# Modulation vectors on VectorE inside the second feed-forward, context work inside that stage and the mixer's

## The reference, cut to what matters

```python
x = x + jnp.square(jax.nn.relu(h @ w_ffn_up[l])) @ w_ffn_down[l]      # end of block 2
...
# start of block 3
sh1, sc1, g1, sh2, sc2, g2 = ada_split(c, w_ada[l], b_ada[l])          # silu(c) @ w_ada + b_ada, six vectors of 1024
csh1, csc1, cg1, csh2, csc2, cg2 = ada_split(c_ctx, w_ada[l], b_ada[l])
u_l, v_l, q_l, k_l, vv_l, o_l, gt_l = split_proj(modulate(x, sh1, sc1) @ w_in[l])
u_c, v_c, q_c, k_c, vv_c, o_c, gt_c = split_proj(modulate(xc, csh1, csc1) @ w_in[l])   # the context, 256 tokens
```

## Time and profile before

| | |
|---|---|
| median of three runs | 4226.23 us (4224.4 to 4230.27) |
| the profiled execution, its own time | 4218.46 us |
| its span, first to last instruction | 4216.7 us |
| mean granted TensorE clock | 0.952 |
| TensorE busy | 3840.2 us (91%) |
| VectorE busy | 2213.2 us (52%) |
| ScalarE busy | 1296.4 us (31%) |
| data moved | 218.14 MB, 52 GB/s on the mean |

### The profile page before, as it was taken

How to read it: one execution, slowest core, us unless ns; L and a number is a source line. 1 busy time by engine, 2 the same in 40 slices (tenths; PEclk the granted TensorE clock), 3 DMA queues, 4 the chain that set the end, 5 groups by cost and what they waited for, 6 DMA issues and landing times. The chain is left out here.

```text
span 4216.7 us, 45629 instructions
## 1 busy us (share of the span) xinstructions
PE 3840.2 (91%) x18134; PEld 3084.2 (73%) x18134; DVE 2213.2 (52%) x3153; ACT 1296.4 (31%) x1902; POOL 157.2 (4%) x95
## 2 busy tenths in 40 slices
PE   6988899999996798787999999988698989999997
PEld 5877778888884686566788888735597756888885
DVE  1087676777776793444434444412636565444446
ACT  1143252222224224434322222212522364222323
POOL 3310000000000000000000000000000000000000
PEclk9998999999998899888999999998899999999998
DMA  2110011111111011000111111162022200111111
GB/s 102 50 61 0 20 40 54 52 45 46 46 50 60 25 51 60 21 0 20 40 60 40 47 54 41 40 233 106 32 65 65 80 30 30 60 40 60 41 51 50
DMA packets 59044, 218.14 MB, mean 52 GB/s; under 512 B 4541, under 2 KB 17085, under 8 KB 53234
## 3 DMA queue, kind: packets, MB, share of 16 engines
q1 hardware_dynamic: 58290, 214.94, 14.1%
q10 hardware_dynamic: 576, 0.72, 0.0%
HBM read 202.97 MB, written 12.65 MB: 51 GB/s over the span
## 5 line engine op out<-in xcount | busy, mean ns | idle before, releaser
L1122 PE MATMUL psum<-mixer_r,pairs_r 128*128 128x512 f32 x2016 | 796.5, 395 | 36.0 <-DVE gemm_input_r L1398 19.4
L1123 PE MATMUL psum<-gemm_input_r,pairs_r 128*128 128x512 f32 x2016 | 788.2, 391 | 0.0
L1124 PE MATMUL psum<-mixer_r,pairs_r 128*128 128x512 f32 x2016 | 788.1, 391 | 0.0
L1156 PE MATMUL psum<-hidden_r,pairs_r 128*128 128x512 f32 x1376 | 543.0, 395 | 27.8 <-DVE residual L1468 13.0
L1157 PE MATMUL psum<-hidden_r,pairs_r 128*128 128x512 f32 x1376 | 539.1, 392 | 0.0
L1158 PE MATMUL psum<-hidden_r,pairs_r 128*128 128x512 f32 x1376 | 539.1, 392 | 0.0
L1468 DVE TENSOR_TENSOR residual<-residual,psum 128x512 f32<-128x512 f32 x592 | 384.0, 684 | 206.6 <-PE psum L1158 205.5
L1122 PEld LDWEIGHTS psum<-mixer_r,pairs_r 128*128 128x128 f32 x2016 | 380.9, 189 | 128.2 <-DVE pairs_r L1393 20.6
L1123 PEld LDWEIGHTS psum<-gemm_input_r,pairs_r 128*128 128x128 f32 x2016 | 381.2, 189 | 81.0 <-issue 2.9
L1124 PEld LDWEIGHTS psum<-mixer_r,pairs_r 128*128 128x128 f32 x2016 | 380.7, 189 | 79.9
L1231 ACT ACTIVATE pairs_r<-pairs 128x2048 fp32r<-128x2048 f32 (+1 forms) x108 | 187.1, 1736 | 793.1 <-DMA pairs<-in_w_up 385.0
(11 more groups left out here) (451 smaller groups left out, 5704.0 us busy)
## 6 DMA issues: line engine op xcount, KB each, us to landing
pairs<-in_w_up SPq DMA_DIRECT2D x38, 1024.0 KB, 7.1
pairs<-in_w SPq DMA_DIRECT2D x32, 1024.0 KB, 5.3
weight_slots<-in_w_ada SPq DMA_DIRECT2D x24, 1024.0 KB, 4.8
pairs<-in_w_down SPq DMA_DIRECT2D x16, 1024.0 KB, 5.2
pairs<-in_w_down SPq DMA_DIRECT2D x22, 512.0 KB, 3.2
pairs<-in_w_in SPq DMA_DIRECT2D x11, 1024.0 KB, 5.2
weight_slots<-in_w_in SPq DMA_DIRECT2D x10, 1024.0 KB, 4.8
pairs<-in_w_out SPq DMA_DIRECT2D x9, 1024.0 KB, 6.0
```

The source lines that it names most:

```text
L1122: pe.matmul(out, w_hi[:, at], c.MR[:, k, halves[n]], start=k == 0, stop=False)
L1123: pe.matmul(out, w_hi[:, at], c.HR[:, k, halves[n]], start=False, stop=False)
L1124: mm = pe.matmul(out, w_lo[:, at], c.MR[:, k, halves[n]], start=False, stop=k == KT - 1)
L1156: pe.matmul(bank, hi, hid(0, ch, n, kd), start=kd == 0, stop=False)
```

## The change

The vectors are made within the second feed-forward: for chunks 3 to 14, one group of 512 columns of `w_ada` each (12 groups), in two parts of 1 MB (four of the eight rows of 128 features). VectorE multiplies each 128 x 512 piece by one number per partition and adds it to an accumulator: four steps a part and vector. Groups 0 to 3 serve both vectors (8 steps a part), groups 4 to 11 only `c`'s (4 steps a part). From group 1 on the first part's steps stand behind the up slab's split, the second part's between the drains 4 to 7 of the first half. TensorE sums over the partitions against a column of ones (8 or 4 matmuls), ScalarE stores the result. The context is normalised in chunk 2, goes to DRAM and comes back at the end of the stage; modulation, gates, keys and values of it are made in the mixer's stage with the slabs that lie there for the latents, as sums of three products. Three stages and their DMAs are gone; `w_ada_3` is laid out by groups.

```diff
+        self.ctx_hi = over("ctx_hi", 47, [P, KT, CTX], F32R)
+        self.ctx_lo = over("ctx_lo", 44, [P, KT, CTX], F32R)
+        self.ctx_norm = nc.dram_tensor("ctx_norm", (P, KT * CTX), F32, kind="Internal").ap()
...
+class ContextSide:
+    FIRST, GROUPS, BOTH = 3, 12, 4
+    def __init__(self, c):
...
+        self.part = [a.rearrange("p a (b n) -> p (a b) n", n=HALF) for a in (c.norm_tiles[0], c.norm_tiles[1][:, 0:2, :])]
+        self.acc = [c.norm_tiles[1][:, 2, 0:HALF], c.norm_tiles[1][:, 2, HALF:]]
...
+        self.steps, at = [], 0
+        for g in range(self.GROUPS):
+            half = 8 if g < self.BOTH else 4
+            self.steps.append((at + half, at + 2 * half))
+            at += 2 * half
+    def group(self, ch):
+        g = ch - self.FIRST
+        return g if 0 <= g < self.GROUPS else None
+    def vectors(self, g):
+        return range(2 if g < self.BOTH else 1)
+    def load(self, sp, g, h):
+        w = self.c.inp["w_ada_3"][g * P:(g + 1) * P, h * SLAB:(h + 1) * SLAB].rearrange("p (k n) -> p k n", n=HALF)
+        sp.dma_start(self.part[h], w).then_inc((self.s["ada_a"], self.s["ada_b"])[h], 16)
+    def gemv(self, dve, g, h, ks=range(4)):
+        width = len(self.vectors(g))
+        n = self.steps[g][h] - (4 - ks[0]) * width
+        dve.wait_ge((self.s["ada_a"], self.s["ada_b"])[h], 16 * (g + 1))
+        if g and not h:
+            dve.wait_ge(self.s["summed"], g)
+        for k in ks:
+            for v in self.vectors(g):
+                w, by = self.part[h][:, k, :], self.cond[:, 4 * h + k, v:v + 1]
+                if k or h:
+                    dve.wait_ge(self.s["gemv"], n + 1 - width)
+                    dve.scalar_tensor_tensor(out=self.acc[v], in0=w, scalar=by, in1=self.acc[v], op0=ALU.mult,
+                                             op1=ALU.add).then_inc(self.s["gemv"], 1)
+                else:
+                    dve.tensor_scalar(self.acc[v], w, by, None, ALU.mult).then_inc(self.s["gemv"], 1)
+                n += 1
+    def sum_up(self, pe, g):
+        pe.wait_ge(self.s["gemv"], self.steps[g][1])
+        n = 4 * len(self.vectors(g))
+        for i in range(n):
+            mm = pe.matmul(self.c.PS[:, 0, i:i + 1], self.acc[i // 4][:, (i % 4) * P:(i % 4 + 1) * P], self.c.ones[:, 0:1],
+                           start=i == 0, stop=i == n - 1, skip_group_check=True)
+        mm.then_inc(self.s["summed"], 1)
+    def keep(self, act, g):
+        n = len(self.vectors(g))
+        act.wait_ge(self.s["summed"], g + 1)
+        act.activation(self.ada[:, 4 * g:4 * g + 4, 0:n], self.c.PS[:, 0, 0:4 * n].rearrange("p (s a) -> p a s", a=4),
+                       ACT.Copy).then_inc(self.s["ada_kept"], 1)
...
             for ch in range(2, N):
                 sp.wait_ge(up_done, up_at[ch - 2, 1, 1])
                 load_up(ch)
+                if side is not None and ch == 2:
+                    sp.wait_ge(A[1][0].s["scaled"], 8)
+                    sp.dma_start(side.x, c.inp["ctx"].rearrange("p (k n) -> p k n", n=CTX)).then_inc(s["ctx_in"], 16)
+                if side is not None and ch == 4:
+                    sp.wait_ge(s["ctx_scaled"], 1)
+                    side.load(sp, 0, 0)
+                    sp.dma_start(c.ctx_norm.rearrange("p (k n) -> p k n", n=CTX), side.sq).then_inc(s["ctx_out"], 16)
+                    sp.wait_ge(s["ctx_out"], 16)
+                    side.load(sp, 0, 1)
+                if side is not None and side.group(ch):
+                    g = side.group(ch)
+                    for h in range(2):
+                        sp.wait_ge(s["gemv"], side.steps[g - 1][h])
+                        side.load(sp, g, h)
...
+            if side is not None:
+                sp.wait_ge(up_done, up_at[E, 1, 1])
+                sp.dma_start(c.PW[:, 8:10, :], c.ctx_norm.rearrange("p (a n) -> p a n", n=T)).then_inc(c.ctx_landed, 16)
+                sp.wait_ge(c.ctx_landed, 16)
...
                 if ch >= 1:
                     pe.wait_ge(up_drained, up_at[ch - 1, n, m])
+                if side is not None and ch == 3 and m == 0:
+                    pe.wait_ge(s["ctx_log"] if n else s["ctx_centred"], 1)
+                if side is not None and ch > 3 and m == n == 0 and side.group(ch - 1) is not None:
+                    pe.wait_ge(s["ada_kept"], side.group(ch - 1) + 1)
...
+                if side is not None and ch == 2:
+                    pe.wait_ge(s["ctx_in"], 16)
+                    pe.wait_ge(up_drained, up_at[2, 0, 0])
+                    for k in range(KT):
+                        mm = pe.matmul(PS[:, 0, 0:CTX], c.ones_d[:, :], side.x[:, k, :], start=k == 0, stop=k == KT - 1)
+                    mm.then_inc(s["ctx_mean"], 1)
+                    down_half(1, 0)
+                    pe.wait_ge(s["ctx_sq"], 1)
+                    pe.wait_ge(up_drained, up_at[2, 1, 0])
+                    for k in range(KT):
+                        mm = pe.matmul(PS[:, 1, 0:CTX], c.ones_d[:, :], side.sq[:, k, :], start=k == 0, stop=k == KT - 1)
+                    mm.then_inc(s["ctx_sums"], 1)
+                    down_half(1, 1)
+                elif side is not None and side.group(ch) is not None:
+                    down_half(ch - 1, 0)
+                    down_half(ch - 1, 1, range(0, 4))
+                    pe.wait_ge(up_drained, up_at[ch, 0, 0])
+                    side.sum_up(pe, side.group(ch))
+                    down_half(ch - 1, 1, range(4, 8))
+                elif not conv:
...
+                    if side is not None and ch == 2:
+                        for v, name in enumerate(("c_3", "c_ctx_3")):
+                            act.activation(side.cond[:, :, v:v + 1], c.vec(name, 0, 8).unsqueeze(2),
+                                           ACT.Silu).then_inc(s["cond_ready"], 1)
                     round_slab("up", ch + 1)
                     evacuate(ch, 0, 0)
                     round_slab("down", ch - 1)
                     evacuate(ch, 0, 1)
                     evacuate(ch, 1, 0)
                     evacuate(ch, 1, 1)
+                    if side is not None and ch == 2:
+                        act.preload_act_table_set("natural_log_exp_and_others")
+                        act.wait_ge(s["ctx_centred"], 1)
+                        act.activation(side.sq, side.x, ACT.Square).then_inc(s["ctx_sq"], 1)
+                        act.wait_ge(s["ctx_sums"], 1)
+                        act.activation(side.rstd, PS[:, 1, 0:CTX], ACT.Ln, bias=c.ln_eps[:, :]).then_inc(s["ctx_log"], 1)
+                        act.wait_ge(s["ctx_log"], 1)
+                        act.activation(side.rstd, side.rstd, ACT.Exp, scale=-0.5).then_inc(s["ctx_rstd"], 1)
+                    if side is not None and side.group(ch) is not None:
+                        side.keep(act, side.group(ch))
...
+                    g = None if side is None else side.group(ch)
                     split_slab("up", ch + 1)
+                    if g:
+                        side.gemv(dve, g, 0)
                     low_hidden(ch, 0, 0)
                     split_slab("down", ch - 1)
                     low_hidden(ch, 0, 1)
                     low_hidden(ch, 1, 0)
+                    if g == 0:
+                        dve.wait_ge(s["cond_ready"], 2)
+                        side.gemv(dve, g, 0)
+                    if side is not None and ch == 2:
+                        dve.wait_ge(s["ctx_mean"], 1)
+                        mean = PS[:, 0, 0:CTX].unsqueeze(1).to_broadcast([P, KT, CTX])
+                        dve.tensor_tensor(side.x, side.x, mean, ALU.subtract).then_inc(s["ctx_centred"], 1)
                     drains(ch - 1, 0, range(0, 3))
                     low_hidden(ch, 1, 1)
-                    drains(ch - 1, 0, range(3, 8))
-                    drains(ch - 1, 1)
+                    for m in range(3, 8):
+                        drain(ch - 1, 0, m)
+                        if g and m >= 4:
+                            side.gemv(dve, g, 1, range(m - 4, m - 3))
+                    if g == 0:
+                        side.gemv(dve, g, 1)
+                    drains(ch - 1, 1, range(0, 4))
+                    if side is not None and ch == 2:
+                        dve.wait_ge(s["ctx_centred"], 1)
+                        dve.wait_ge(s["ctx_rstd"], 1)
+                        rstd = side.rstd.unsqueeze(1).to_broadcast([P, KT, CTX])
+                        dve.tensor_tensor(side.sq, side.x, rstd, ALU.mult).then_inc(s["ctx_scaled"], 1)
+                    drains(ch - 1, 1, range(4, 8))
             if not conv:
                 split_slab("down", E - 1)
+            if side is not None:
+                dve.wait_ge(s["ada_kept"], side.GROUPS)
...
-def block3_ada(c, prefetch):
...
-def block3_context(c, prefetch):
...
-    units = [("gate", 0, n) for n in range(2)]
-    units += [(w, m, n) for w in "qk" for m in range(2) for n in range(2)]
-    units += [(w, t) for w in ("vals0", "vals1", "v0") for t in range(NC_)]
```

(75 more changed lines are left out.)

156 lines of the change are left out of this document (40 added, 116 removed).

## The result

The changed kernel takes **4109.02 us** (median of four runs, 4106.36 to 4114.25), the kernel before in the same session 4227.85 (4224.4 to 4230.27): a ratio of **0.9721, with a 95% interval of 0.9704 to 0.9738**. The forecast was 4121, range 4103 to 4142. The profiled execution of the changed kernel took 4110.98 us with a span of 4109.2, that of the kernel before 4218.46 and 4216.7. So the spans differ by -107.5 us where the sum said -105.0, and the medians by -118.8.

The account below looks back on a forecast made before the run. TensorE, busy 91% of the span, was taken as the bound; -153.5 + 0.6 + 6.9 + 16.6 + 3.2 + 21.2 = -105.0 us gave 4113.5 us, and 7.8 from execution to median gave 4121 us, range 4103 to 4142.

Parts of the forecast that it names:

- Removed stages: Between feed-forward and the latents' layer norm: three stages go, boundaries included, -153.5 us.
- Chunks: Second feed-forward: TensorE's added context statistics, sums, clock loss and group 0's lateness, +27.3 us.
- the sum over partitions: Feed-forward chunks: 128 one-column TensorE instructions at 0.13 us each, 16.6 us, between 7.7 and 27.
- a clock that should fall behind two of the four long sums: Feed-forward chunks with two vectors: TensorE's clock falls behind two of four sums, 3.2 us.
- VectorE's steps and its margins: Feed-forward chunks: steps of 0.66 to 0.79 us lie beside TensorE, costing 0, with 1.5 us of cover; group 0 excepted.
- rival C: Feed-forward chunks: VectorE holds TensorE up, about 10 us over four chunks at 1.0 us a step, 4131 us; chance 0.12.
- Rival B: Feed-forward chunks: the clock falls behind every sum, 19.2 us in place of 3.2, 4137 us; chance 0.10.
- Rival E: Feed-forward, SyncE's queue: late second parts delay the next slabs in every chunk, slower than before, 4241 us; chance 0.02.
- Rival D: Feed-forward sums: small matmuls at their lower bound and no clock fall, 8.9 + 3.2 us better, 4109 us; chance 0.12.
- Layer norm: The latents' layer norm stage after the feed-forward: no change expected, 0 us.
- Mixer: Mixer stage: context units 20.2 us, later gate split 1.2, cheaper evacuation -0.2, together +21.2 us.
- VectorE modulates eight tiles, 0.3 us each: Mixer's start: eight 128 x 256 modulation steps ahead of the gate slab's split make it 1.2 us later.

Follow-up runs that it names:

- second profile: The changed kernel run and profiled once more with no edit, the base for the small edits: 4108.84 us, ratio 0.9732 to the kernel before.
- the doubled sum: Every sum over partitions computed twice in the changed kernel: 4131.88 us in one piece, 4125.32 us with two down units between.
- the experiment: The changed kernel with ScalarE loading another table set at the end of the second feed-forward: 4114.66 us, 5.8 above the unedited kernel in the same session.
- first profile: The changed kernel's original profiled execution, no edit: 4110.98 us, with a span of 4109.2 us.

## Why the prediction came out right, and where it did not

**Removed stages.** -153.5 expected, -154.8 measured. The 1.3 us beside it are clock: the tail's last six float32 matmuls took 3.53 us after and 4.76 before, and VectorE waited 5.1 us for what follows them (6.3 before). Over the kernels above this tail varies from 0.8 us less to 1.3 more than in the changed kernel's second profile, with the same instructions.

**Chunks.** +22.9 against +27.3. Chunk 2 cost 7.0 (6.9 expected) and group 0's late block 0.9 (0.6). The step that was mis-sized is the sum over partitions: I took 0.13 us an instruction from the row with ten moving columns, and the doubled sum measures 0.116, so 14.8 us and not 16.6. The floor between starts that the Trainium skill gives ("TensorE: Matmul & The Clock Gate", section "Back-to-back issue gap") is not reached: 0.116 us is over four times it. The same section says that such gaps leave the weight loads out, and in the trace each of the 128 instructions has a weight load of 128x128, so these sums could not be expected to reach the floor. That the loads set the 0.116 was not tried. And I counted 3.2 us for a clock that should fall behind two of the four long sums; it stayed at 1.00 behind all twelve. The clock does fall for such stretches: it stayed behind 1.85 us of small matmuls between large ones, fell behind 3.7 us in all four chunks, and behind 1.85 us with a wait of 0.7 ahead in three of four.

**VectorE's steps and its margins.** Timed to 0.7 us everywhere: +16.7 for +17.3, +19.6 for +20.3, +36.3 for +36.6. The first end came 0.6 early because two of its eight steps are plain products of 0.4 us each. The margins are real (twelve steps in place of eight cost 2.25 us a chunk at full clock, about the 2.4 that rival C reckoned for steps of 1.0 us), so C was rightly a rival and failed only because a step takes 0.66 us. **Half of the steps between the drains** is what keeps the sum from being late; as a block it would have cost 0.9 us in each of three chunks and, what I had not seen, the clock as well, 2.5 in all. Rival B fell with the clock at 1.00. Rival E fell with the slabs issued at every chunk's begin. Rival D has the measured median to the microsecond (4109), and that is luck: of its two halves the clock came true (3.2 us), the small matmuls at 0.06 us (8.9) did not.

**Layer norm.** 0 expected, -2.1 measured. The step that failed is an omission: of the removed stages I counted the work, and not the table set that they left behind. Behind their last Silu ScalarE loaded four tables in the layer norm and one in the mixer; all five are gone. Some of the 2.1 may be clock, as the experiment says. By the Trainium skill ("ScalarE: Activation LUTs", section "What ACT_TABLE_LOAD costs") each takes about 1283 ns, which is what every row here shows.

**Mixer.** +24.7 against +21.2. (In the first profile it was +30.2, over the 27 that the prediction named as a sign that it is wrong; 5.6 of that is the clock at its end.) The context's units cost the 20.2 us of the forecast. The gate slab's split came 6.2 us later and not 1.2: the term that failed is "VectorE modulates eight tiles, 0.3 us each". Alone a step takes 0.33 us; five of the eight stood beside GpSimd's five memsets and took 1.33, one memset's length each. The first of these memsets was in the trace before too (2983.16, beside a TENSOR_TENSOR, which it did not slow), and I had not asked what the new operation shares with it. The Trainium skill ("SBUF — State Buffer", section "Who interferes with whom") has the rule: a TENSOR_SCALAR can take the port pair that VectorE shares with GpSimd, and whoever holds it keeps it for a whole instruction; the trace agrees. Against this stands the k slab's wait, 1.5 us where I left it at 3.0, since the table load in the way of ScalarE's exponentials is gone.

**The 12 us between forecast and median.** 2.5 are the sum. In the first profile the chunks came 4.4 us under it, the layer norm 2.2, the tail 1.3, and clock ahead of the feed-forward and behind the mixer 3.6; the mixer came 9.0 over it, 5.6 of that by the clock at its end. So that the sum came so near is in part luck: errors of 11.5 us one way stand against 9.0 the other. The other 9.8 are the step from execution to median. I added 7.8 us because the median of before stood so far above its profile; the changed kernel's stood 2.0 below its own. The runs of the kernel before reach from 4214 to 4231 us over the sessions, and its two profiles differ by 3.7 us, nearly all of it by clock. The offset of one execution belonged in the range and not in the forecast. The ends of that range do not follow from their terms either: D and half of the 7.8 us give 4105 and not 4103, and the costliest rival taken one at a time gives 4137 and not 4142. The measured median lies within the narrower range too.

## What to carry to other kernels

A float32 matmul instruction with one moving column cost 0.116 us here, as long as large matmuls stood close on both sides; keep such stretches short, break a long one with a large unit, and let nothing be waited for ahead of it. When a step moves to another engine or place, ask who else is active there at that moment: the same eight steps cost 7.3 us beside GpSimd's memsets and 2.7 us, all hidden, in a wait of VectorE at the end of the stage before. And when a stage is removed, look at the state that it left (a table set, a clock level) as well as at its work.

## What was not expected of the hardware

VectorE's 128x256 TENSOR_SCALARs and GpSimd's 36x1280 memsets took turns, 1.33 us a step in place of 0.33, while in the kernel before a TENSOR_TENSOR of 128x1024 beside the same memsets kept its 1.23 us. TensorE's granted clock fell to half behind 3.7 us of back-to-back one-column matmuls though the engine was never idle (50.33 us busy of 50.33, clock 0.93), and at one place of the same kernel it fell in one execution and not in the next: at the mixer's end it was 0.67 and 1.00. Such falls come and go in pieces of 1.3 to 5.6 us and make most of the spread between executions that the profiles show. What decides between the two was not tried.
